# The first down projection of a two-block transformer kernel: sixteen of its 22 row blocks as two sets of seven products

## The reference

```python
def _conv_gated_mlp(h, w_up, conv_w, conv_b, w_down):
    hid = h @ w_up                              # 512 x 5632
    hid = depthwise_conv_of_width_3(hid, conv_w) + conv_b
    a, b = jnp.split(hid, 2, axis=-1)
    return (jax.nn.gelu(a) * b) @ w_down        # (512 x 2816) @ (2816 x 1024)

h2 = _rmsnorm(x, g_pre_ffn)
x = x + _rmsnorm(_conv_gated_mlp(h2, w_up, conv_w, conv_b, w_down), g_post_ffn)
```

## Time and profile before

| | us |
|---|---|
| median of 3 runs | 1567.03 (1566.85 to 1567.38) |
| the profiled execution | 1569.01 |
| its span, first to last instruction | 1566.9 |
| PE busy | 1550.7 |
| DVE / POOL / ACT busy | 914.3 / 725.1 / 533.1 |

### The profile page before, as it was taken

How to read it: one execution, slowest core, us unless ns; L and a number is a source line. 1 busy time by engine, 2 the same in 40 slices (tenths; PEclk the granted TensorE clock), 3 DMA queues, 4 the chain that set the end, 5 groups by cost and what they waited for, 6 DMA issues and landing times.

```text
span 1566.9 us, 19248 instructions
## 1 busy us (share of the span) xinstructions
PE 1550.7 (99%) x7495; PEld 1279.0 (82%) x7495; DVE 914.3 (58%) x1185; ACT 533.1 (34%) x760; POOL 725.1 (46%) x289
## 2 busy tenths in 40 slices
PE   9999999999999999999999999999999999999997
PEld 6887788888888988888888897887778988888886
DVE  5901589820074566666301578997764436585878
ACT  3012211210124434344213435227643343333444
POOL 5875189687762254444544001441124263645551
PEclk9999999999999999999999999999999999999999
DMA  6242023233234223333224032331124164536462
GB/s 229 81 134 81 1 88 107 68 121 108 81 108 134 81 81 108 92 95 107 84 105 142 29 108 60 103 96 40 28 82 153 37 187 137 146 91 184 88 188 81
DMA packets 132885, 159.57 MB, mean 102 GB/s; under 512 B 5527, under 2 KB 98759, under 8 KB 132808
## 3 DMA queue, kind: packets, MB, share of 16 engines
q1 hardware_dynamic: 125430, 141.05, 28.4%
q0 software_dynamic: 5504, 12.58, 4.5%
q10 hardware_dynamic: 1874, 4.85, 0.9%
HBM read 152.18 MB, written 2.10 MB: 98 GB/s over the span
## 4 chain that ended last, share of the span: by engine, by line
PE 86%; POOL 6%; issue 4%; DVE 2%; ACT 2%; DMA 1%; POOLq 0%; DVEq 0%; SPq 0%; ACTq 0%
PE ps L849 26%; PE ps L850 26%; PE ps L851 26%; PE ps L1004 3%; PE ps L1079 2%; POOL w_lo L834 1%; PE ps L1246 1%; POOL w_lo L773 1%; PE ps L1067 1%; POOL w_lo L832 1%; PE ps L1263 1%; POOL tail_lo L834 1%; POOL w_hi L768 1%; PE ps L1138 1%; POOL tail_lo L832 0%
## 5 line engine op out<-in xcount | busy, mean ns | idle before, releaser
L773 POOL TENSOR_TENSOR w_lo<-raw,w_hi 128x1024 fp32r<-128x1024 f32 x166 | 420.5, 2554 | 497.8 <-ACT w_hi L1349 495.0
L849 PE MATMUL ps<-hT_hi,w_hi 128*128 128x512 f32 (+1 forms) x848 | 325.2, 383 | 1.1 <-POOL w_lo L773 0.5
L850 PE MATMUL ps<-hT_lo,w_hi 128*128 128x512 f32 (+1 forms) x848 | 323.7, 382 | 0.0
L851 PE MATMUL ps<-hT_hi,w_lo 128*128 128x512 f32 (+1 forms) x848 | 323.6, 382 | 0.0
L768 POOL TENSOR_TENSOR w_hi<-raw,cells 128x2048 fp32r<-128x2048 f32 x35 | 129.6, 3703 | 126.3 <-PE ps L849 125.2
L849 PEld LDWEIGHTS ps<-hT_hi,w_hi 128*128 128x128 f32 x848 | 159.7, 188 | 34.6 <-issue 2.3
L851 PEld LDWEIGHTS ps<-hT_hi,w_lo 128*128 128x128 f32 x848 | 159.7, 188 | 30.9
L850 PEld LDWEIGHTS ps<-hT_lo,w_hi 128*128 128x128 f32 x848 | 159.8, 188 | 30.1
L1349 ACT ACTIVATE w_hi<-raw 128x2048 fp32r<-128x2048 f32 (+1 forms) x58 | 109.7, 1891 | 128.6 <-PE ps L849 106.5
L849 PE MATMUL ps<-w_hi,hT_hi 128*128 128x512 f32 (+2 forms) x400 | 151.6, 379 | 0.5 <-POOL w_lo L792 0.5
L850 PE MATMUL ps<-w_lo,hT_hi 128*128 128x512 f32 (+2 forms) x400 | 150.1, 375 | 0.0
(11 more groups left out here) (368 smaller groups left out, 3054.3 us busy)
## 6 DMA issues: line engine op xcount, KB each, us to landing
raw<-in_w_in SPq DMA_DIRECT2D x86, 512.0 KB, 4.6
raw<-in_w_up SPq DMA_DIRECT2D x54, 512.0 KB, 4.7
raw<-in_w_down SPq DMA_DIRECT2D x38, 512.0 KB, 4.5
raw_tail<-in_w_up SPq DMA_DIRECT2D x22, 512.0 KB, 4.7
raw<-in_w_out SPq DMA_DIRECT2D x16, 512.0 KB, 4.2
raw_tail<-in_w_down SPq DMA_DIRECT2D x16, 512.0 KB, 5.8
raw<-in_w_ret_o SPq DMA_DIRECT2D x8, 512.0 KB, 4.0
raw<-in_w_sgu_o SPq DMA_DIRECT2D x8, 512.0 KB, 4.1
```

The source lines that it names most:

```text
L773: nc.gpsimd.tensor_tensor(lo[:, c], raw[:, s, c], hi[:, c].bitcast(f32), ALU.subtract).then_inc(unit_split, 1)
L849: first = nc.tensor.matmul(dst, a_hi, b_hi, start=start, stop=False, skip_group_check=onto)
L850: nc.tensor.matmul(dst, a_hi, b_lo, start=False, stop=False, skip_group_check=onto)
L851: return first, nc.tensor.matmul(dst, a_lo, b_hi, start=False, stop=stop, skip_group_check=onto)
```

## The change

The first 16 row blocks of w_down (2048 rows, `FS = 16`) become two sets of seven products. The last 6 blocks (768 rows) stay plain, three units of which the last two are joint.

- PE: 14 calls of `set_product` take the place of eight units. Product 6 of a set goes on in the banks of product 5, product 3 in those of product 0, product 4 in those of product 2.
- The results of the sets are gathered in `h_added`. For products 0, 2, 3 and 6 of the first set ACT copies (`set_copy`), all others DVE adds (`set_take`).
- w_up units 0 to 15 no longer split f: the gate writes `f` directly. Units 16 to 21 still make `f_hi` and `f_lo`. ACT's and DVE's steps of the last unit, 21, are spread over the first set.
- SP loads four blocks per set, POOL issues T1, T3 and T4 as in the tail.
- The two gain vectors are loaded after the sets (their place holds tokens until then).
- The boundary becomes `"summed"`: in step A DVE first adds both banks of the tile onto `h_added`, ACT squares the sum from there, and DVE scales it in one instruction.

Core of the diff (what PE, DVE and ACT do in the sets, the two new orders, the new step A):

```diff
+SET_W = (2, 0, 1, 2, 0, 1, 2, 0, 1, 2, 1, 0, 2, 1)
+COPIED = tuple((0, n) for n in (0, 2, 3, 6))
...
+            def set_product(v):
...
+                await_set_low(pe, v)
+                pe.wait_ge(set_a_lo, v + 1)
+                for t in range(2):
+                    b = set_bank(2 * v + t)
+                    used = [e for e in range(2 * v + t) if set_bank(e) == b]
+                    if used:
+                        await_set_taken(pe, used[-1])
...
+            for at_v in range(SET_N):
+                set_product(at_v)
...
+            long("down1", (FB - FS) // 2, f_hi, f_lo, ready=lambda k: pe.wait_ge(f_made, FS + k + 1),
+                 after="h3", free=set_free)
...
             # POOL
+            for v in range(SET_N):
+                q, n = divmod(v, 7)
+                if n == 1:
+                    await_set_loaded(pool, q, "B11")
+                    await_set_low(pool, 7 * q)
+                    set_sum(q, "T1", set_block(q, 0, 1))
+                elif n == 2:
+                    await_set_loaded(pool, q, "B12")
+                    set_sum(q, "T3", set_block(q, 1, 1))
+                elif n == 4:
+                    await_set_low(pool, 7 * q + 1)
+                    await_set_sum(pool, q, "T2")
+                    set_sum(q, "T4", set_raw[SET_RAW[q]["B11"]].rearrange("p (k n) -> p k n", k=4))
+                if set_low(v)[0]:
+                    continue
...
             # ACT
+            for at_v in range(SET_N):
+                if at_v:
+                    set_copy(2 * at_v - 1)
+                if at_v + 2 < SET_N:
+                    set_token_high(at_v + 2)
+                    set_high(at_v + 2)
+                set_copy(2 * at_v)
+                if at_v == 1:
+                    up_centre(FB - 1)
+                elif at_v == 3:
+                    up_gelu(FB - 1)
+                elif at_v == 5:
+                    up_high(FB - 1)
...
             # DVE
+            set_token_low(0)
+            set_token_sum(0, "S3")
+            set_token_sum(0, "S1")
+            set_token_low(1)
+            for at_v in range(SET_N):
+                q, n = divmod(at_v, 7)
+                if at_v:
+                    set_take(2 * at_v - 1)
+                if n < 2:
+                    set_token_sum(q, TOKEN_SUMS[2 + n])
+                if n >= 5 and q + 1 < SETS:
+                    set_token_sum(q + 1, TOKEN_SUMS[n - 5])
+                if n == 1:
+                    set_weight_sum(q)
+                if at_v + 2 < SET_N:
+                    set_token_low(at_v + 2)
+                    if set_low(at_v + 2)[0]:
+                        set_weight_low(at_v + 2)
+                set_take(2 * at_v)
+                if at_v == 2:
+                    up_taps(FB - 1)
+                elif at_v == 4:
+                    up_gate(FB - 1, kept=False)
+                elif at_v == 6:
+                    up_low(FB - 1)
...
             # ACT, boundary, step A
+                    if which == "A" and kind == "summed":
+                        for half in range(2):
+                            await_evacuated(act, tin + 2 * tt + half)
+                        step.up(nc.scalar.activation(h_rows[:, :, tok], h_added[:, :, tok], ACT.Square,
+                                                     accum_out=sq[:, 0:1]))
...
             # DVE, boundary, step A
+                    if which == "A" and kind == "summed":
+                        for half in range(2):
+                            t = tin + 2 * tt + half
+                            row = h_added[:, 4 * half:4 * half + 4, tok]
+                            await_psum(dve, t)
+                            V.tensor_tensor(row, row, bank(t).rearrange("p (k n) -> p k n", k=4),
+                                            ALU.add).then_inc(evacuated[BANK[t]], 1)
+                        rms_in.take()
...
+                        step.up(V.scalar_tensor_tensor(added, added, rstd[:, c:c + 1],
...
+                        V.tensor_tensor(row, row, added, ALU.add).then_inc(x_added, 1)
```

More of the change, by code:

```diff
@@ L9 @@
 KT = D // P
+SETS = 2
+FS = SETS * 8
 RET_H, RET_DK, RET_DV = 4, 128, 256
@@ new lines, in set_copy @@
+            def set_copy(e):
+                if divmod(e // 2, 7) in COPIED:
+                    act.wait_ge(set_ready, e + 1)
+                    row, half = set_row(e)
+                    nc.scalar.activation(row, set_psum(e), ACT.Copy, scale=-1.0 if half else 1.0).then_inc(set_copied, 1)
+            for j in range(4):
+                up_centre(j)
+                if j:
+                    give_hi(U0["up1"] + j + 2)
+                up_gelu(j)
+            with act.Fori(1, FS // 4) as i:
+                for j in range(4):
+                    up_centre(j, i)
+                    give_hi(U0["up1"] + j + 2, i, 4)
+                    up_gelu(j, i)
@@ L1533, in _ @@
+            act.wait_ge(set_started, SET_N)
+            load_gain(0, a["g_post_ffn"])
+            load_gain(1, a["attn_norm"])
+            for u in range(U0["down1"] + 1, U0["kv_iq"] + 2):
                 if u == U0["kv_iq"]:
@@ new lines, in up_low, with set_take @@
+            def up_low(j):
+                dve.wait_ge(f_hi_made, j - FS + 1)
+                V.tensor_tensor(f_lo[:, j - FS:j - FS + 1, :], taps[:, j % 2, 0:1, :],
+                                f_hi[:, j - FS:j - FS + 1, :].bitcast(f32), ALU.subtract).then_inc(f_made, 1)
+            def set_take(e):
+                if divmod(e // 2, 7) not in COPIED:
+                    row, half = set_row(e)
+                    first = [w for w in range(e) if TO_X[w // 2 % 7] == TO_X[e // 2 % 7] and w % 2 == e % 2]
+                    if first:
+                        await_set_taken(dve, first[-1])
+                    dve.wait_ge(set_ready, e + 1)
+                    V.tensor_tensor(row, row, set_psum(e), ALU.subtract if half else ALU.add).then_inc(set_added, 1)
```

290 lines of the change are left out of this document (247 added, 43 removed).

## The result

The changed kernel takes 1569.43 us (median of 20 runs, 1569.02 to 1572.05) against 1567.29 us for the kernel before (20 runs beside it). The ratio is 1.0015, with a 95% interval from 1.0008 to 1.0021. That is 2.1 us more.

A forecast was written before the change was run, and what follows sets the result against it. TensorE, busy 99% of the span, was taken as the bound: -10.88 us for 48 matmuls, +6.8 sets, +7.4 boundary = +3.3 us on 1567.03, giving 1570.3 us; forecast 1568.5 to 1573 (chance 0.48), wider range 1565 to 1575.

The forecast's parts named there:

- the sets: In the fourteen products, waits on DVE and POOL plus restarts were to cost 6.8 us, from 2.8 to 12.
- the boundary: Between w_down and the next block, additions before ACT's square make tiles 8.9 us; cost 7.4 us with late weights.
- the middle class: Whole-kernel time between 1563.9 and 1570.2 us, not told from no change; chance 0.37.
- The saving and the entry: In w_down, 48 fewer matmuls save 10.88 us; product 0's preparation is covered by w_up unit 21, costing nothing.
- Product 6: In the sets, it waits for DVE's take behind S3 and a token low slowed by POOL: 2.8 us.
- rival 1: Sets run at the tail's pace if DVE reaches S3 before POOL's half: sets cost 2.8, 1566.4 us; chance 0.27.
- Product 10: In the second set, a chain from low 7 through T1's transfer to DVE's low makes it wait 2.3 us.
- Products 4 and 11: In the sets, both wait for POOL's weight lows: 0.3 us and 1.0 us.
- The last kv_iq weights land a little later than now: At the boundary, their slot is freed by a split following the sets: 0 to 0.6 us, taken as 0.1.
- Tile 0: At the boundary, its rows were to be ready 2.5 us after PE wanted to transpose them.
- The hidden boundary: PE would not feel the longer boundary tiles: 1564 us, or 1560 with the sets at the tail's pace; chance 0.12.
- rival 3: In the sets, POOL keeps the port through both halves, DVE falls behind for good: sets about 12, 1575.5 us; chance 0.13.

The follow-up runs named there:

- take first: The changed kernel with DVE's take of product 5's first half moved ahead of the token sum and token low for product 7; 1571.59 us.
- no additions: The changed kernel with the boundary tiles normalised straight from the accumulators, leaving out DVE's eight additions of the products' sum; 1562.65 us.
- low 7 on DVE: The changed kernel with product 7's weight low made by DVE instead of POOL, and DVE's and ACT's steps reordered around it; 1567.73 us.
- lows 7 and 11: The changed kernel with the weight lows of products 7 and 11 made by DVE instead of POOL; 1568.50 us.
- both, late low: The changed kernel with product 7's and 11's weight lows on DVE, boundary additions earlier, and the next projection's second weight low behind tile 1's second normalisation; 1561.12 us.
- filled waits: The changed kernel with unused matmuls added, ten ahead of product 6 and sixteen ahead of tile 0's transposes; 1569.73 us.
- additions ahead: The changed kernel with the same boundary additions placed earlier in DVE's order, tile t+1's ahead of tile t's second normalisation; 1562.90 us.
- both repairs: The changed kernel with the weight lows of products 7 and 11 on DVE and the boundary additions moved earlier in DVE's order; 1561.56 us.

## Why the prediction was right, and where it was not

The time, 1570.3 us predicted and 1569.43 measured, came from two large terms that were both about right; that they erred in opposite directions, the sets 1.0 us too dear and the boundary 0.8 too cheap in the profiled execution, is luck. The most likely sign was not: 0.50 stood on slower by over 0.2%, and the measured 0.15% lies in the middle class.

**The saving and the entry.** Right: 48 matmuls less, and no wait ahead of product 0.

**The sets: 6.8 predicted, 5.8 measured** (5.7 where the clock kept up).

- Product 6, 2.8 predicted, 2.56 measured. The mechanism, a DVE step caught beside POOL's low 7, is right, the instruction is not: S3 was to take some 3 us and took 1.22, which the prediction itself had named as a sign of error. Counted from product 5's start (780.40), DVE came free at 2.7 us instead of 3.1 and POOL began at 3.4 instead of 3.0. So rival 1's condition (S3 ahead of POOL) was met by 0.7 us, but it was drawn one step too early: the token low, too, must be ahead. That the size came out near is in part luck: one step of 1.1 us less stood behind POOL's first half, but that half ended at 6.2 us instead of 5.3. The run with the take first shows how sharp this edge is.
- Product 10, 2.3 predicted. The chain from the end of low 7 (789.9) to product 10 (812.14) is 22.26 us against 22.2 in the working. The loss is 1.8 us where the clock stayed up (no additions) and 0.3 in the profiled execution, since there product 6's slow matmuls gave the chain 1.7 us. The reading that it hangs on the issue of T1 was half wrong: issued 4 us sooner it left a wait of 2.02 us. DVE's order ahead of T2's sum holds it, and the run that moved that sum (and the f block's low) removed it.
- Products 4 and 11, 0.3 and 1.0 predicted, 0.3 (products 4 and 5 together) and 0.8 measured.

**The boundary: 7.4 predicted, 8.2 measured** in the profiled execution (7.7 to 8.0 in the four other runs with the same boundary, by the table's column less 47.0). The mechanism, ACT's square no longer beside the tile before, is right: without the additions the time falls by 6.8 us. A tile takes 8.65 us, not 8.9; the additions were taken from takes at 1.39 and took 1.28. Tile 0 was mis-sized: 2.5 predicted, 3.9 measured. The failed step is "The last kv_iq weights land a little later than now", taken at 0.1 us: ACT waited 2.10 us for them, and the lows ended 1.7 us later against the joint units. Moving that low away gives 0.8 us (boundary 48.36 to 47.53). Tiles 1 and 3 lost 2.3 and 1.85 us, against 2.5 and 2.3; of tile 1's loss only 0.47 us is a wait, the rest is the slow matmuls ahead of it.

**The rivals.** The hidden boundary is excluded by the 8.2 us that PE lost there, 6.8 of which came back without the additions. DVE falling behind did not come, though its row did: POOL kept the port through both halves (6.23 us). It fell on an instruction for which nobody waited; with S1 in that place it cost. That POOL's low stands right behind a transfer, as rival 3 has it, does not settle it: low 8 stood so in the run with low 7 on DVE too, and there two steps of DVE were held for one half each (3.43 and 2.88 us). ("SBUF — State Buffer", section "Who interferes with whom", in the Trainium skill has the lock last one whole instruction; 6.23 and 7.29 us over two POOL instructions differ, 3.42 us agree.)

**What was missing** is the clock. The sum came out right without it, since behind both drops stood a wait that took it up. With the waits filled the stretches give -10.9 + 5.6 + 7.7 = +2.4 us, which is what that kernel's median lies above the kernel before (1569.73 to 1567.32); the +3.3 of the profiled execution, the same as the forecast, is in part its own scatter.

## What to carry to other kernels

A step that is added to a chain between two engines belongs in the time in which the chain already waits for the other one: here the same eight additions cost 6.8 us in one order and 0.25 in the other. Where two engines contend, look not only at the instruction that you added but at which one stands there once it has moved, and at giving the work to the engine that is faster at it (2.3 us on DVE, 6 on GpSimd, plus what it no longer blocks). Before one wait of TensorE is removed, follow what it hides: three times here the next wait took its place, until the order on DVE was right.

## What the runs showed of the hardware

- Behind a wait of TensorE of 2.0 to 3.8 us up to nine matmuls may run 0.43 us apart instead of 0.23 (granted clock 0.50 in the 4 us from 860 in the run with low 7 on DVE). Each kernel was profiled in one execution. The drop came behind 2.40 and 3.76 us (the change), 2.56 and 3.29 (take first), 3.38 (low 7), 2.02 and 3.60 (lows 7 and 11), 2.02 (both, late low) and 1.97 us (filled waits), and not behind 2.40 and 1.67 (no additions; 2.39 and 1.69 with the additions ahead) or 2.02 (low 7, both repairs). What decides stays open.
- A wait of 2 us is not needed for it: the far drop, between 1056 and 1076 us, came with no wait over 0.4 us ahead, in four of the thirteen profiled executions, though those waits stand in all of them.
- It costs 1.6 us of the median behind product 10, where nothing behind takes it up, and nothing that could be measured where something does. Matmuls whose results nobody uses kept the clock up at all three places where they filled a wait; at product 10 the five runs then lay within 0.07 us.
- Takes, which read one operand from PSUM, were not held up beside POOL: two took 1.27 us together at 816.02 in the changed kernel, while POOL's low 11 ran from 812.60 to 818.36 and the token lows on either side, with both operands in SBUF, took 2.89 and 2.22 us instead of 1.2.
